# Routing of a hierarchical MoE by token block, with the two blocks' chains alternating on VectorE

## What is computed

```python
pg = softmax(t @ w_rg); pg_top, g_idx = top_k(pg, 1)                 # 4 groups
le = (t @ w_re).reshape(-1, 4, 8); le_sel = le[g_idx]                # 8 experts of the group
pe_top, e_idx = top_k(softmax(le_sel), 2)
w = pg_top * pe_top / sum(pe_top);  ids = g_idx * 8 + e_idx
combine = sum(one_hot(ids, 32) * w)                                  # per token, 32 experts
a = silu(h @ w_gate[e]) * (h @ w_up[e]) * combine[e];  out = sum_e a @ w_down[e]
```

## Time and profile before

| what | value |
|---|---|
| median of 3 runs | 1031.8 us (1031.7 to 1032.82) |
| the profiled execution | 1031.66 us, its span 1029.6 us |
| busy, share of the span | PE 93%, PEld 65%, DVE 56%, ACT 42%, POOL 6% |
| moved by DMA | 313.02 MB, mean 304 GB/s |
| chain that ended last, by engine | PE 71%, DMA 11%, SPq 9%, DVE 4%, ACT 3% |
| routing, layer 1 and layer 2 | around 313 to 320 us and 821 to 828 us |

### The profile page before, as it was taken

The page is one execution under the profiler, slowest core; times in us unless marked ns, Lnnn a source line. Parts: engine busy times, 40 slices in busy tenths (PEclk is TensorE's granted clock), DMA queues, the critical chain, the costliest instruction groups (busy, mean ns, idle before and its releaser), DMA issues.

```text
span 1029.6 us, 15478 instructions
## 1 busy us (share of the span) xinstructions
PE 960.6 (93%) x5906; PEld 670.6 (65%) x5906; DVE 573.9 (56%) x1182; ACT 429.4 (42%) x912; POOL 58.0 (6%) x74
## 2 busy tenths in 40 slices
PE   9999999999999995986999999999999999978777
PEld 7888777778886442532588887777888954344323
DVE  7656888886873231210276668898868533222212
ACT  5444566666444210210354355666764441111122
POOL 1120400000010000000004004000000100000000
PEclk9999999999999999998999999999999999989989
DMA  9975533247999999999998655332589999999996
GB/s 347 348 251 179 197 123 124 82 122 272 397 368 388 424 426 419 425 423 427 413 392 275 203 187 181 123 123 82 169 294 385 363 411 425 424 422 423 425 424 273
DMA packets 97113, 313.02 MB, mean 304 GB/s; under 512 B 13424, under 2 KB 18576, under 8 KB 74512
## 3 DMA queue, kind: packets, MB, share of 16 engines
q1 hardware_dynamic: 96704, 312.04, 79.7%
q10 hardware_dynamic: 336, 0.02, 0.0%
HBM read 310.20 MB, written 1.84 MB: 303 GB/s over the span
## 4 chain that ended last, share of the span: by engine, by line
PE 71%; DMA 11%; SPq 9%; DVE 4%; ACT 3%; issue 2%; POOL 0%; DVEq 0%; POOLq 0%; ACTq 0%
PE ps L1414 14%; PE ps L1416 14%; PE ps L1415 14%; SPq L484 8%; PE ps L2038 6%; DMA arena<-in_w_expert_up_dram 5%; DMA arena<-in_w_expert_gate_dram 3%; DMA ring_rest<-in_w_expert_down_dram 3%; PE ps L2124 2%; PE ps L2012 2%; PE ps L1439 2%; PE ps L2112 2%; PE ps L1537 2%; PE ps L1549 2%; PE ps L1983 1%
## 5 line engine op out<-in xcount | busy, mean ns | idle before, releaser
L1414 PE MATMUL ps<-whi,ahi 128*128 128x512 f32 (+1 forms) x736 | 284.6, 387 | 2.2 <-DVE wlo L1080 2.0
L1080 DVE TENSOR_TENSOR wlo<-arena,whi 128x512 fp32r<-128x512 f32 (+1 forms) x352 | 232.8, 700 | 93.7 <-ACT whi L883 91.7
L1416 PE MATMUL ps<-whi,alo 128*128 128x512 f32 (+1 forms) x736 | 277.0, 376 | 0.0
L1415 PE MATMUL ps<-wlo,ahi 128*128 128x512 f32 (+1 forms) x736 | 276.7, 376 | 0.0
L883 ACT CAST whi<-arena 128x1024 fp32r<-128x1024 f32 (+1 forms) x175 | 179.6, 1029 | 183.4 <-PE ps L1416 177.2
L1414 PEld LDWEIGHTS ps<-whi,ahi 128*128 128x128 f32 x736 | 138.5, 188 | 32.6 <-DVE wlo L1080 4.7
L1416 PEld LDWEIGHTS ps<-whi,alo 128*128 128x128 f32 x736 | 138.4, 188 | 25.9
L1415 PEld LDWEIGHTS ps<-wlo,ahi 128*128 128x128 f32 x736 | 138.7, 188 | 23.1
L2256 DVE SCALAR_TENSOR_TENSOR acts<-ps,wslot,acts 128x256 f32<-128x256 f32 x16 | 7.7, 483 | 173.7 <-ACT acts L1939 149.1
L2038 PE MATMUL ps<-arena,rows 128*32 128x512 f32 x416 | 91.7, 625 | 8.8 <-DMA arena<-in_w_expert_up_dram 6.9
L2038 PE MATMUL ps<-ring_rest,rows 128*32 128x512 f32 x352 | 77.6, 643 | 12.7 <-DMA arena<-in_w_expert_up_dram 12.7
(11 more groups left out here) (292 smaller groups left out, 1071.2 us busy)
## 6 DMA issues: line engine op xcount, KB each, us to landing
arena<-in_w_in_dram SPq DMA_DIRECT2D x62, 1024.0 KB, 5.3
arena<-in_w_expert_down_dram SPq DMA_DIRECT2D x38, 1024.0 KB, 20.6
arena<-in_w_expert_gate_dram SPq DMA_DIRECT2D x34, 1024.0 KB, 25.9
arena<-in_w_expert_up_dram SPq DMA_DIRECT2D x32, 1024.0 KB, 25.3
ring_rest<-in_w_expert_down_dram SPq DMA_DIRECT2D x24, 1024.0 KB, 18.9
ring_rest<-in_w_expert_gate_dram SPq DMA_DIRECT2D x22, 1024.0 KB, 25.9
ring_rest<-in_w_expert_up_dram SPq DMA_DIRECT2D x22, 1024.0 KB, 26.0
arena<-in_w_proj_a_dram SPq DMA_DIRECT2D x8, 1024.0 KB, 5.2
```

Source lines behind the costliest of these rows:

```text
L1080: dve.tensor_tensor(wlo[:, jj % 2, cols], half_slot(jj, w)[:, cols], whi[:, jj % 2, cols].bitcast(F32), ALU.subtract).then_inc(low_split i ...
L1414: pe.matmul(o, hi, rhs_hi, start=first, stop=False)
L1415: pe.matmul(o, hi, rhs_lo, start=False, stop=False)
L1416: return pe.matmul(o, lo, rhs_hi, start=False, stop=last)
```

## The change

The router's products and what follows them are split by token block.

- The logits of block tb stand in bank 4 + tb. The transposes of k = 6 and 7 go to four banks, one per (k, block): (7, 3) and (6, 2). Each is evacuated in 128 columns, k = 6 on ScalarE and k = 7 on VectorE. TensorE finishes block 0's products before block 1's, and signals each.
- VectorE handles each block with its own chain, the two alternating by hand. A step waits for its own predecessor's count, not for the instruction before it. Experts are chosen over all 32: the logits of the other groups are lowered by 3e38, then one `max` and one `max_index` over 32 give the two experts, and `pick` is 32 wide. `sel` is the sum of the two picks. The mean and reciprocal of the norm stand between steps of block 1.
- `sel` of each block raises `picked`; ranks come per block, from banks 6 and 4, and `rank` is called in `build` for quad 0, before the one-hot of the block.
- 3 fillers instead of 7 follow the router's products. `idx_iota` is 32 wide. The weights are multiplied into `pick` in place, and `comb` is the sum of the two.
- Waits: the first router part waits for both early evacuations ahead of k = 0; the last transposes wait for the third evacuation of ScalarE.

```diff
-        WARM_SETUP, WARM_ROUTE, WARM_RANKS, WARM_LAST = 7, 7, 1, 1
+        WARM_SETUP, WARM_ROUTE, WARM_RANKS, WARM_LAST = 7, 3, 1, 1
...
+        def turned_last(k, tb):
+            return ps[:, ((7, 3), (6, 2))[k - (KB - 2)][tb], 0:P]
...
-                if k == 2 or k == KB - 1:
-                    pe.wait_ge(h2t_odd, 1 if k == 2 else 2)
-                elif k % 2 == 0:
-                    pe.wait_ge(h2t_ready, part + 1)
-                for tb in range(TB):
-                    mm = pe.matmul(ps[:, 4, tb * 64:tb * 64 + WR], h2t[:, k, tb * P:(tb + 1) * P], wr[:, k, 0:WR],
+                for tb in blocks:
+                    if k == 0 or k == KB - 1:
+                        pe.wait_ge(h2t_odd, 2 + tb if k else 1)
+                    if k % 2 == 0 and k != 2:
+                        pe.wait_ge(h2t_ready, 3 + tb if part == 2 else part + 1)
+                    mm = pe.matmul(ps[:, 4 + tb, 0:WR], h2t[:, k, tb * P:(tb + 1) * P], wr[:, k, 0:WR],
...
-                router_part(pe, 1, (5,))
-                router_part(pe, 2)
+                for tb in range(TB):
+                    router_part(pe, 1, (5,), (tb,))
+                    router_part(pe, 2, blocks=(tb,))
                 keep_clock(pe, WARM_ROUTE)
 
                 pe.wait_ge(picked, 1)
-                pe.matmul(ps[:, 6, 0:EXPERTS], before[:], sel[:, 0, :], start=True, stop=True)
...
+                pe.matmul(ps[:, 6, 0:EXPERTS], before[:], sel[:, 0, :], start=True, stop=True).then_inc(ranks_ready, 1)
+                pe.matmul(ps[:, 4, 0:EXPERTS], ones[:], sel[:, 0, :], start=True, stop=False)
+                pe.matmul(ps[:, 7, 0:EXPERTS], ones[:], sel[:, 0, :], start=True, stop=False)
+                pe.wait_ge(picked, 2)
+                pe.matmul(ps[:, 4, 0:EXPERTS], before[:], sel[:, 1, :], start=False,
                           stop=True).then_inc(ranks_ready, 1)
...
+                step0 = copied(0)
+                step0 = best_group(0, step0)
+                step0 = group_index(0, step0)
+                step0 = other_groups(0, step0)
+                step0 = lower(0, step0)
+                step1 = copied(1)
+                step0 = best_experts(0, step0)
+                step1 = best_group(1, step1)
+                step0 = expert_index(0, step0)
+                step1 = group_index(1, step1)
+                step0 = picks(0, step0)
+                step1 = other_groups(1, step1)
+                selected(0, step0)
+                step1 = lower(1, step1)
                 dve.wait_ge(squares, 2)
...
+                step1 = best_experts(1, step1)
...
+                step1 = expert_index(1, step1)
...
+                step1 = picks(1, step1)
+                selected(1, step1)
...
                     for tb in range(TB):
+                        if n == 0 and not routed:
+                            rank(dve, link, tb)
```

More of the change, by code:

```diff
@@ L552, in turned_new @@
         def turned_new(k):
[L554 to L556 removed]
+            at = (k % 2) * S
+            return ps[:, 4 + k // 2, at:at + S]
+        def turned_last(k, tb):
+            return ps[:, ((7, 3), (6, 2))[k - (KB - 2)][tb], 0:P]
         def h2t_act(act, l, i):
             act.wait_ge(x_turned, i + 1)
[L560 removed]
+            for k in (2 * i, 2 * i + 1):
                 last = act.activation(h2t[:, k, :], turned_new(k), ACT.Copy, scale=second_gain(l, k))
@@ L582, in turn_new_x @@
         def turn_new_x(pe, part, blocks=range(TB)):
+            if part == 2:
+                pe.wait_ge(h2t_ready, 2)
             for tb in blocks:
@@ L585, in turn_new_x, with router_part @@
                 for k in X_PARTS[part]:
-                    mm = pe.transpose(turned_new(k)[:, tb * P:(tb + 1) * P], xs[:, tb, k * P:(k + 1) * P], ident[:])
-                    if tb and k % 2:
+                    to = turned_last(k, tb) if part == 2 else turned_new(k)[:, tb * P:(tb + 1) * P]
+                    mm = pe.transpose(to, xs[:, tb, k * P:(k + 1) * P], ident[:])
+                    if (tb or part == 2) and k % 2:
                         mm.then_inc(x_turned, 1)
-        def router_part(pe, part, ks=None):
+        def router_part(pe, part, ks=None, blocks=range(TB)):
             if part == 0:
@@ L1767, in route_pe @@
                 turn_new_x(pe, 2, (1,))
-                router_part(pe, 1, (5,))
-                router_part(pe, 2)
+                for tb in range(TB):
+                    router_part(pe, 1, (5,), (tb,))
+                    router_part(pe, 2, blocks=(tb,))
                 keep_clock(pe, WARM_ROUTE)
                 pe.wait_ge(picked, 1)
-                pe.matmul(ps[:, 6, 0:EXPERTS], before[:], sel[:, 0, :], start=True, stop=True)
-                pe.matmul(ps[:, 6, 64:64 + EXPERTS], before[:], sel[:, 1, :], start=True, stop=False)
-                pe.matmul(ps[:, 6, 64:64 + EXPERTS], ones[:], sel[:, 0, :], start=False,
+                pe.matmul(ps[:, 6, 0:EXPERTS], before[:], sel[:, 0, :], start=True, stop=True).then_inc(ranks_ready, 1)
[3 more added lines that the diff above has]
+                pe.matmul(ps[:, 4, 0:EXPERTS], before[:], sel[:, 1, :], start=False,
                           stop=True).then_inc(ranks_ready, 1)
-                pe.matmul(ps[:, 7, 0:EXPERTS], ones[:], sel[:, 0, :], start=True, stop=False)
                 pe.matmul(ps[:, 7, 0:EXPERTS], ones[:], sel[:, 1, :], start=False,
@@ L1836, in route_dve, with rank @@
                                   ALU.subtract).then_inc(router_in, 1)
-                dve.wait_ge(ranks_ready, 1)
-                ranks = ps[:, 6, 0:2 * 64].rearrange("p (t n) -> p t n", t=TB)[:, :, 0:EXPERTS]
-                link(dve.tensor_tensor(rk[:], ranks, sel[:].bitcast(F32), ALU.mult))
+            def rank(dve, link, tb):
+                dve.wait_ge(ranks_ready, tb + 1)
+                link(dve.tensor_tensor(rk[:, tb, :], ps[:, 4 if tb else 6, 0:EXPERTS], sel[:, tb, :].bitcast(F32),
+                                       ALU.mult))
             def combine_weights(dve, link):
```

124 lines of the change are left out of this document (70 added, 54 removed).

## The result

The changed kernel took **1035.91 us** (median of 6 runs, 1035.43 to 1037.1); the kernel before beside it took 1031.99 (1031.4 to 1032.82). The ratio is 1.0039 [1.0029, 1.0049]: 3.9 us slower, where 1.5 us faster was forecast. The profiled execution took 1035.73 us, its span is 1034.0.

The account below looks back on a forecast made before the run. The weight stream at 422 GB/s was taken as the bound, with routing deciding only when loads are released. Releases 1.0 us earlier gain 0.85 us in layer 1 and 0.7 in layer 2, total 1.5: 1030.3 us, range 1029.3 to 1032.3.

Parts of the forecast that it names:

- What bounds the kernel: Expert stage: weight loads at 422 GB/s bound it; routing matters only through load releases, whose holes are worth 1.80 us together.
- Parts 1 to 3: Routing: block logits 1.0 and 0.27 us earlier, second sel 0.8 us earlier, first gather taken as 1.0 us earlier per layer.
- Part 3: Ranks and one-hots: first gather at 318.95 instead of 320.11, taken as 1.0 us per layer; wider iota below 0.05 us.
- Part 4: GpSimd's copies beside VectorE's block 0 steps: taken as nothing; a held comparison costs 0.4 us, leaving a 0.75 us shift.
- The sum: Weight stream: releases 1.0 us earlier close layer 1's first hole; 0.85 us gained there, 0.7 in layer 2, total 1.5 us.
- Rival B: Holes in the weight stream: slow flow belongs to those transfers, not the empty queue; nothing passes, 1031.5 to 1032.1; chance 0.14.
- Rival D: TensorE in routing: fewer fillers leave it idle, its clock drops from 2.4 to 1.2 GHz; 1033.0 to 1036.2; chance 0.07.
- Rival C: VectorE's alternating chains: no overlap between instructions, gather 0.8 us late per layer, 1033.4; chance 0.06.
- rival A: Weight stream: the whole release shift passes to the layer's end, 2.0 to 2.3 us gained, 1029.5 to 1029.8; chance 0.17.

Follow-up runs that it names:

- e1: Kernel before with only 96 unused bytes per partition behind idx_iota, shifting every buffer behind it: 1035.22 us, ratio 1.0033.
- f2: Changed kernel with 160 unused bytes behind idx_iota, so ring_rest is at a multiple of 256 B again: 1032.97 us, ratio 1.0012.
- f4: Changed kernel with all weight slots on multiples of 256 B, four fillers after the router and two before block 1's counting products: 1030.92 us, ratio 0.9994.
- f1: Kernel before with pads of 96 bytes ahead of arena and 160 behind idx_iota, all 20 weight slots on multiples of 256 B: 1029.5 us, ratio 0.9982.
- h2: f4 with SyncE alone holding the first released load until TensorE's second pair of gathers: 1029.46 us, ratio 0.9976.
- f3: f2 with four fillers after the router and two ahead of block 1's counting products, to hold TensorE's clock: 1033.22 us, ratio 1.0013.
- e2: Changed kernel with 32 unused bytes behind idx_iota, putting ring_rest at a multiple of 128 B: 1036.2 us, ratio 1.0043.
- h3: Changed kernel at its own addresses with two fillers before the first gather: 1036.01 us, ratio 1.0036.
- i2: Changed kernel at its own addresses with f4's fillers, clock held and release at 9.32 us: 1036.46 us, ratio 1.0037.
- e4: Changed kernel at its own addresses with seven fillers after the router instead of three: 1036.26 us, ratio 1.0052.
- g2: f4 with one more filler before the first gather, 0.47 us of delay: 1029.0 us, ratio 0.9965.
- g1: f4 with two more fillers before the first gather, 0.9 us of delay: 1028.66 us, ratio 0.9971.

## Why the prediction was wrong, step by step

**What bounds the kernel**: right that the weight stream bounds it and that routing matters only through it. Wrong in that the full rate was taken as given; it was the term that moved most.

**Parts 1 to 3**: right. Block 0's copy 314.62 (314.76 forecast), second sel 317.86 (317.90), first gather 319.11 (318.95), 1.0 us earlier in layer 1. In Part 3, "The wider iota is set up once, below 0.05 us" is the step that failed by the most: nothing shows of the instruction, but its 96 B cost 3.4 us (e1), 2.8 by the difference of the changed kernel and f2. The sum had no term for what the diff moves in SBUF.

**Part 4**: taken at nothing, and it showed. The 4-element comparison took 0.40 us beside GpSimd's copy, which ended at 315.68, and 0.16 behind it, and the gather came 0.16 us later than forecast. The shift of 1.0 us lies between the two ends of 1.15 and 0.75, and nothing hung on it.

**The sum**: "Releases come 1.0 us earlier. Layer 1: the first hole closes" failed. The release of layer 2 did come 0.9 us earlier and the hole did not close (213 GB/s for 246; 11.52 MB in 30 us for 11.79); with aligned slots the early release cost 1.4 us (f4 against f1) instead of bringing 1.5, and holding that load alone brought them back (h2). The reasoning took a load's flow to begin a fixed 2 us after its issue; with the early issue most engines' first packets ended 4.0 us after it (layer 1 of f3). Rival B (nothing passes) was nearest in mechanism. What stood against it, that both layers show the hole at the same distance from the release, could not tell a dry queue from a slow first packet; and its price, 1031.5 to 1032.1, had no loss in it.

**Rival D**, the clock, came true in one layer of three kernels. Of the eight layers profiled with three fillers, the granted clock fell to 0.50 (1.2 GHz) in three (after, layer 1; e2, layer 2; h3, layer 1), after idle times of only 0.36 and 0.60 us between single small products; the other five kept 1.00 with like idle times (0.35 and 0.60 in f2, layer 1), and it fell in none of the other 30 layers. The condition "it decides from the idle length" was too simple, since a time of 3.51 us had been the only row. Its price was right at the lower end: the release came 0.6 us later than before (10.81 for 10.21). But a release at 10.8 moves no less than one at 9.3 (11.58 and 11.52 MB), so by itself it cost nothing that shows: i2, with the clock held, is at 1.0037 beside the 1.0039 of the change, and e4 at 1.0052. That the measured 1035.91 lies in rival D's 1033.0 to 1036.2 is luck.

Rival C did not occur (315.74 and 315.84 overlap on VectorE), and rival A had the wrong sign. Of the 3.9 us, then, 2.8 to 3.4 are the addresses; the 0.5 to 1.2 left fit the early release (f2, at the rate of before, is 1.2 us slower than the kernel before), but at the change's own addresses that is not resolved.

## What to carry to other kernels

Where a DMA stream is the bound, a diff must also be read for what it moves in memory: look where each buffer that the stream fills now begins, and try a pad before anything else is explained. Here pads alone made the kernel before 1.9 to 2.4 us faster (f1). And an earlier issue is not an earlier landing: with the queue still 2 us deep, the time gained ahead of the stream was worth less than nothing, and giving half or all of it back (g2, g1) made the fastest kernels here, 3.0 to 3.6 us below the kernel before by the ratios and 7 us below the change. Most of that is the alignment (f1) and the release put back; none of it is shown to be the new routing.

## What was not expected of the hardware

A packet of 8192 B takes 309 ns, almost without exception, when every slot begins on a multiple of 256 B, and 311 to 318 ns in most cases when none does; a multiple of 128 B does not help (1036.2 us, e2). Unaligned loads right behind aligned ones kept the short packets (94% of the first two), which they did not when no slot was aligned (8%). With a load issued 9.3 us behind four others of 1 MB the stream moves 0.25 MB less in the 30 us from their issue than with one issued 9.5 to 10.4 us behind them. TensorE's granted clock fell to half after two idle times of 0.36 and 0.60 us in 3 of 8 layers, and in none of the 30 layers with six or seven fillers around them. A 4-element operation of VectorE on two SBUF operands took 0.40 us beside GpSimd's copy, to within 0.02 us of the copy's end, and 0.16 us behind it.
